# A state-space and attention trunk on one core: the normalization of P from ScalarE to GpSimd

## The chip, the cores and the metric

The kernel runs on one core of a Trainium2 chip. The metric is the device time of one execution in microseconds (us); the median of several runs is compared. The core has five engines with their own instruction streams: TensorE (PE; its weight loads are the rows PEld), VectorE (DVE), ScalarE (ACT), GpSimd (POOL) and SyncE (SP, which only issues transfers here). They run ahead of one another freely and meet through semaphores. An engine works off its stream in order: an instruction that waits holds up all behind it on that engine.

## The reference

512 tokens of 1024 features go through two layers, in float32. Layer 0 is an S5 state-space mixer with a gated projection, then an MLP with squared ReLU (1024 to 4096 to 1024). Layer 1 is sliding-window attention with 16 query heads of 64 over 4 shared key/value heads, then such an MLP, then a final RMSNorm. What the change touches is this part:

```
for each block of 128 queries (4 blocks), against its own and the previous block of keys:
    s = q @ k.T / 8                 # masked to a causal window of 128
    m = maximum(max(s), sink)
    p = exp(s - m)
    denom = sum(p) + exp(sink - m)
    o = (p / denom) @ v
out = o @ w_o + b_o
```

The division p / denom is the normalization that is moved.

## The kernel before, in words

Every large product is made in units. A unit is one panel of 1024 x 128 weights against all 512 tokens. Its 24 matmuls of 128x512 (lines 1110 to 1112, or 1074 to 1076) take each of 8 tiles three times: the weights are split into a high part `w_hi` and a low part `w_lo`, the activations likewise. There are 164 units in a fixed order; PE counts each finished one in `unit_done`. SP brings the panels into two buffers `raw`. POOL makes the two parts, in `split(u, s)`: a tiny `gate()` (line 341), a copy with rounding into `w_hi` (line 414), and after that has landed `w_lo = raw - w_hi` (line 417). There are four slots for the parts, so split u waits until unit u - 4 is done (`unit_done >= u - 3`). Before the change the splits 4 to 163 are one loop on POOL, and POOL does nothing else from unit 4 on.

Attention stands between the units of keys and values (80 to 83), the query units (84 to 91, names `U_Q` and on) and the output units (92 to 99, `U_O` and on). It is cut into 16 steps that the code calls Q, from 0 to 15: Q // 4 says which 4 heads, n = Q % 4 which block of queries. For n = 0 there is no previous block, so a head has 128 keys there and 256 in all other steps. `q = Q % 2` is the buffer. A step has these parts:

- PE `scores(Q)` (line 1205): 8 small matmuls into PSUM. They wait until DVE has read the scores of step Q - 1 (`s_masked`).
- DVE `maxima(Q)`: writes the sink logit into a column of `s_sb` (line 921), adds the mask (line 923), takes the row maximum (929) and negates it (931).
- ACT `exps(Q)` (line 572): one exponential for each of 4 heads, with its row sum.
- DVE `denominators(Q)` (line 936): the reciprocal `rden` of the 4 sums; it counts `rden_done`.
- ACT `norm_p(Q)` (line 579): for each of 4 heads a copy of `s_sb` in place with the per-row scale `rden`; it counts `p_norm`.
- PE `turn_p(Q)` (line 1217): transposes P once `p_norm` has all four counts of the step.
- ACT and DVE `turned(Q)` (lines 585 and 941): each moves half of the transposed P from PSUM to SBUF.
- PE `mix(Q)` (line 1231): P times V. Then ACT `o_hi` (line 591) and DVE `o_low` (line 947) split the result.

The function `skewed` writes the parts out, each engine with its own lags. In pass Q, PE does scores(Q), then dense work that stands beside it, then mix(Q - 2), then turn_p(Q - 1). ACT does turned(Q - 2), o_hi(Q - 3), norm_p(Q - 1), exps(Q). DVE does turned(Q - 2), denominators(Q - 1), maxima(Q), o_low(Q - 3), and in even passes up to 10 the next queries (lines 908 and 910). The dense work is half a query unit (12 matmuls) in each of the passes 0 to 10, half an output unit in passes 11 and 12, none in 13 to 15, and three quarters of a unit each in 16 and 17. Query unit 2 + Q/2 is finished in even pass Q; that is what releases split 90 + Q/2.

Of the kernel before, what the change touches and what calls it, by code (L numbers as in the profile page):

```python
# [11 lines left out]
ACT = mybir.ActivationFunctionType  # L12
# [5 lines left out]
KT = D // P  # L18
# [18 lines left out]
NBLK = L // BLK  # L37
QUADS = 4
# [6 lines left out]
U_Q = U_KV + 4  # L45
U_O = U_Q + KT
NU = U_MLP[1] + 2 * NB_FF * KT
# [50 lines left out]
def build(nc, panels, xu_d, x_d, lam_d, prm_d, dd_d, cst_d, mask_d, col_d, out_d):  # L98
    ctx = ExitStack()
    with ctx:  # L100
        def sb(name, shape, dt=F32, where=ctx):
            return where.enter_context(nc.sbuf_tensor(name, shape, dt))

        def sem(name):
            return ctx.enter_context(nc.semaphore(name))
# [92 lines left out]
        s_sb = sb("s_sb", [P, 2, 4, 2 * BLK + 1], where=over)  # L198
# [4 lines left out]
        rden = sb("rden", [P, 2, 4], where=over)  # L203
# [31 lines left out]
        p_exp, rden_done, p_norm = sem("p_exp"), sem("rden_done"), sem("p_norm")  # L235
# [39 lines left out]
        def window(n):  # L275

            return slice(BLK if n == 0 else 0, 2 * BLK)
# [57 lines left out]
        def _(pool):  # L335
            mul, add, sub = ALU.mult, ALU.add, ALU.subtract
# [73 lines left out]
            def split(u, s):  # L410
                pool.wait_ge(raw_in[s % 2], 16 * (u // 2 + 1) if isinstance(u, int) else 8 * (u - s) + 16 * (s // 2 + 1))
                wait(pool, unit_done, u - 3)
                gate()
                nc.gpsimd.tensor_scalar(w_hi[:, s, :], raw[:, s % 2, :], 1.0, 0.0, ALU.mult, ALU.add  # L414
                                        ).then_inc(w_hi_done, 1)
                pool.wait_ge(w_hi_done, u + 1)
                nc.gpsimd.tensor_tensor(w_lo[:, s, :], raw[:, s % 2, :], w_hi[:, s, :].bitcast(F32),  # L417
                                        ALU.subtract).then_inc(w_split, 1)
# [4 lines left out]
            wait(pool, st_done, 2 * NO)  # L423
            split(2, 2)
            split(3, 3)
            with pool.Fori(1, NU // 4) as i:
                for s in range(4):
                    split(4 * i + s, s)

# [2 lines left out]
        def _(a):  # L432
            act_fn = nc.scalar.activation
# [138 lines left out]
                    act_fn(s_sb[:, q, j, at], s_sb[:, q, j, at], ACT.Exp, bias=negm[:, q, j:j + 1],  # L572
                           accum_out=den[:, q, j:j + 1]).then_inc(p_exp, 1)

            def norm_p(Q):
                u, n, q = Q // NBLK, Q % NBLK, Q % 2
                a.wait_ge(rden_done, Q + 1)
                for j in range(4):
                    act_fn(s_sb[:, q, j, window(n)], s_sb[:, q, j, window(n)], ACT.Copy,
                           scale=rden[:, q, j:j + 1]).then_inc(p_norm, 1)  # L580

            def turned(Q):
                u, n, q = Q // NBLK, Q % NBLK, Q % 2
                a.wait_ge(pt_mm, Q + 1)
                act_fn(pT[:, q, 0:2].rearrange("p t b n -> p t (b n)")[:, :, window(n)],
                       ps[:, 4, :].rearrange("p (t m) -> p t m", t=2)[:, :, window(n)], ACT.Copy).then_inc(pt_a, 1)

            def o_hi(Q):
# [3 lines left out]
                       ps[:, 6 + q, 0:256].rearrange("p (t n) -> p t n", t=2),  # L592
                       ACT.Copy).then_inc(ot_hi, 1)

            skewed([(turned, 2), (o_hi, 3), (norm_p, 1), (exps, 0)])

            with a.Fori(0, KT) as m:
                norm_hi(H_O + 1 + m, m, [("g_mlp1", act)])
# [666 lines left out]
def skewed(stages):  # L1265

    last = QUADS * NBLK
    longest = max(lag for _, lag in stages if lag is not None)  # L1270
    for Q in range(last + longest):
        for stage, lag in stages:
            if lag is None:
                stage(Q)
            elif 0 <= Q - lag < last:
                stage(Q - lag)
# [110 lines left out]
```

## Time and profile before

| what | value |
|---|---|
| median of 3 runs | 1096.73 us (1095.37 to 1097.85) |
| the profiled execution | 1094.58 us, its span 1092.8 us |
| PE busy | 1036.5 us, 95% of the span |
| POOL busy | 721.2 us, 66% |
| DVE busy | 627.4 us, 57% |
| ACT busy | 208.9 us, 19% |

The span is the part of the execution that the profile covers. The attention steps run from 585 us (first scores) to 686 us (last mix); the rest of the span is the state-space part, the gated projection and the two MLPs. A row of a group of instructions tells how many there are and how long one takes; a row of the timeline is one instruction, or several alike in a row; what stands in brackets is how long the engine sat idle before it and which instruction ended that. An idle time with "issue" has no releaser in the profile.

### The profile page before, as it was taken

What the parts mean: (1) busy time and instruction counts of PE and PEld (TensorE: products, weight loads), DVE (VectorE), ACT (ScalarE), POOL (GpSimd) and SP (SyncE); (2) the same over time, 40 slices, a digit from 0 to 9 for tenths busy, and PEclk for the clock granted to TensorE, in tenths of its full rate; (3) what the DMA queues carried; (4) which work ended last, traced back from release to release, by engine and by line L of the source; (5) the groups of instructions that cost most, each with busy time, mean ns of one, the idle gap of its engine ahead of it and who ended that gap; (6) DMA issues with size and microseconds to landing.
All of it is one profiled execution on the core that took longest, in us unless ns stands there. A gap on an engine that the chain in (4) does not pass through costs nothing.

```text
span 1092.8 us, 15893 instructions
## 1 busy us (share of the span) xinstructions
PE 1036.5 (95%) x5640; PEld 845.7 (77%) x5640; DVE 627.4 (57%) x715; ACT 208.9 (19%) x455; POOL 721.2 (66%) x563
## 2 busy tenths in 40 slices
PE   4889999999999999999989998969999999999995
PEld 1778888888888888888877776858888888888884
DVE  7997575687316415615945885767771372273164
ACT  4763121111001000001202776111110010010000
POOL 6997787597667667767845320767776676676650
PEclk9799999999999999999999998989999999999998
DMA  6113332232222222222212110122322222222211
GB/s 239 33 30 98 104 113 96 77 116 96 97 96 97 96 96 97 97 96 97 96 62 93 43 55 1 59 96 78 115 96 97 97 96 97 96 96 97 96 58 77
DMA packets 34863, 97.50 MB, mean 89 GB/s; under 512 B 11136, under 2 KB 11648, under 8 KB 34560
## 3 DMA queue, kind: packets, MB, share of 16 engines
q1 hardware_dynamic: 34816, 96.85, 26.1%
q8 instruction: 33, 0.54, 0.2%
q14 instruction: 14, 0.11, 0.0%
HBM read 92.37 MB, written 2.10 MB: 86 GB/s over the span
## 4 chain that ended last, share of the span: by engine, by line
PE 84%; DVE 9%; issue 3%; ACT 1%; POOL 1%; DMA 1%; DVEq 1%; SPq 0%
PE ps L1110 24%; PE ps L1111 24%; PE ps L1112 24%; PE ps L1074 2%; PE ps L1075 2%; PE ps L1076 2%; PE ps L1217 1%; PE ps L1231 1%; PE ps L1205 1%; DVE t L803 1%; DVE act L809 1%; ACT s_sb L572 1%; DMA prm<-prm_in 1%; DVE h L963 1%; DVE h L980 0%
## 5 line engine op out<-in xcount | busy, mean ns | idle before, releaser
L417 POOL TENSOR_TENSOR w_lo<-raw,w_hi 128x1024 fp32r<-128x1024 f32 x164 | 421.3, 2569 | 13.7
L1110 PE MATMUL ps<-hid,w_hi 128*128 128x512 f32 x736 | 289.2, 393 | 1.9 <-issue 1.9
L1112 PE MATMUL ps<-hid,w_lo 128*128 128x512 f32 x736 | 287.1, 390 | 0.0
L1111 PE MATMUL ps<-hid,w_hi 128*128 128x512 f32 x736 | 287.0, 390 | 0.0
L341 POOL TENSOR_TENSOR gate_sb<-gate_sb 128x1 f32<-128x1 f32 x164 | 42.8, 261 | 316.6 <-PE ps L1112 270.8
L1110 PE MATMUL ps<-act,w_hi 128*128 128x512 f32 x464 | 180.7, 389 | 2.3 <-DVE act L809 2.3
L414 POOL TENSOR_SCALAR w_hi<-raw 128x1024 fp32r<-128x1024 f32 x164 | 182.8, 1114 | 0.0
L1112 PE MATMUL ps<-act,w_lo 128*128 128x512 f32 x464 | 180.5, 389 | 0.0
L1111 PE MATMUL ps<-act,w_hi 128*128 128x512 f32 x464 | 180.5, 389 | 0.0
L868 DVE TENSOR_TENSOR h<-ps,h 128x512 f32 x64 | 44.1, 690 | 227.5 <-PE ps L1112 227.5
L1110 PEld LDWEIGHTS ps<-hid,w_hi 128*128 128x128 f32 x736 | 138.5, 188 | 34.7 <-issue 5.2
L1112 PEld LDWEIGHTS ps<-hid,w_lo 128*128 128x128 f32 x736 | 138.5, 188 | 29.1
L1111 PEld LDWEIGHTS ps<-hid,w_hi 128*128 128x128 f32 x736 | 138.6, 188 | 28.2
L857 DVE TENSOR_TENSOR hid<-t,hid 128x512 fp32r<-128x512 f32 x64 | 129.2, 2019 | 44.7 <-ACT hid L552 44.7
L552 ACT ACTIVATE hid<-t 128x512 fp32r<-128x512 f32 x64 | 40.5, 633 | 455.6 <-DVE t L855 455.6
L1110 PEld LDWEIGHTS ps<-act,w_hi 128*128 128x128 f32 x464 | 87.1, 188 | 20.9 <-DVE act L809 2.7
L1112 PEld LDWEIGHTS ps<-act,w_lo 128*128 128x128 f32 x464 | 87.1, 188 | 18.0
L1111 PEld LDWEIGHTS ps<-act,w_hi 128*128 128x128 f32 x464 | 87.1, 188 | 18.0
L853 DVE SCALAR_TENSOR_TENSOR t<-ps,rstd 128x512 f32<-128x512 f32 x64 | 44.1, 689 | 55.2 <-PE ps L1112 54.7
L855 DVE TENSOR_TENSOR t<-t 128x512 f32<-128x512 f32 x64 | 67.1, 1048 | 2.2
L806 DVE TENSOR_TENSOR acc<-acc,t 128x512 f32<-128x512 f32 x32 | 62.9, 1967 | 3.2
L526 ACT ACTIVATE act<-h,col x24 | 17.4, 724 | 143.3 <-DVEq L870 78.7
(200 smaller groups left out, 1011.9 us busy)
## 6 DMA issues: line engine op xcount, KB each, us to landing
raw<-panels_in SPq DMA_DIRECT2D x164, 512.0 KB, 3.2
xy<-xu_in SPq DMA_DIRECT2D x4, 512.0 KB, 7.9
out<-h SPq DMA_DIRECT2D x8, 256.0 KB, 2.0
prm<-prm_in SPq DMA_DIRECT2D x1, 1280.0 KB, 5.8
h<-x_rows_in SPq DMA_DIRECT2D x1, 1280.0 KB, 13.1
h<-x_rows_in SPq DMA_DIRECT2D x1, 768.0 KB, 7.3
dd<-dd_in SPq DMA_DIRECT2D x1, 256.0 KB, 6.2
toep<-k_even SPq DMA_DIRECT2D x4, 64.0 KB, 2.3
```

Source lines behind the costliest of these rows:

```text
L341: nc.gpsimd.tensor_tensor(gate_sb[:, 0:1], gate_sb[:, 1:2], gate_sb[:, 1:2], ALU.mult)
L414: nc.gpsimd.tensor_scalar(w_hi[:, s, :], raw[:, s % 2, :], 1.0, 0.0, ALU.mult, ALU.add).then_inc(w_hi_done, 1)
L417: nc.gpsimd.tensor_tensor(w_lo[:, s, :], raw[:, s % 2, :], w_hi[:, s, :].bitcast(F32), ALU.subtract).then_inc(w_split, 1)
L552: act_fn(hid[:, par, 0, m, :], t2[:, m % 2, :], ACT.Copy).then_inc(hid_hi, 1)
L806: tt(acc[:], acc[:], t1[:], ALU.add).then_inc(sq_acc, 1)
L853: stt(t1[:], ps[:, m % 4, :], 0.0, rstd[:], ALU.max, ALU.mult).then_inc(bank_free, 1)
L855: tt(t2[:, m % 2, :], t1[:], t1[:], ALU.mult).then_inc(hid_sq, 1)
L857: tt(hid[:, par, 1, m, :], t2[:, m % 2, :], hid[:, par, 0, m, :].bitcast(F32), ALU.subtract).then_inc(hid_lo, 1)
L868: tt(tile(h, m), ps[:, s, :], tile(h, m), ALU.add).then_inc(bank_free, 1)
L1110: mm(ps[:, bank, :], w_hi[:, s, w], x[:, 0, k, :], start=(k == 0), stop=False)
L1111: mm(ps[:, bank, :], w_hi[:, s, w], x[:, 1, k, :], start=False, stop=False)
L1112: last = mm(ps[:, bank, :], w_lo[:, s, w], x[:, 0, k, :], start=False, stop=(k == KT - 1))
```

## The change

The four copies with a scale of `norm_p` leave ACT and become four `tensor_scalar` multiplications on POOL, with the same `rden` as a per-row scalar. For this, POOL's loop over splits is cut at attention: the splits 4 to 83 stay a loop, 84 to 89 are written out, then come 16 passes, each with norm_p(Q) and, in the even passes 0 to 10, split 90 + Q/2 in front of it; the splits 96 to 163 are a loop again. ACT's order in a pass becomes turned(Q - 2), o_hi(Q - 3), exps(Q). PE and DVE keep their streams; turn_p(Q) waits for the same count, which POOL now gives.

```diff
-            with pool.Fori(1, NU // 4) as i:
+            with pool.Fori(1, U_Q // 4) as i:
+                for s in range(4):
+                    split(4 * i + s, s)
+
+            def norm_p(Q):
+                n, q = Q % NBLK, Q % 2
+                pool.wait_ge(rden_done, Q + 1)
+                for j in range(4):
+                    nc.gpsimd.tensor_scalar(s_sb[:, q, j, window(n)], s_sb[:, q, j, window(n)], rden[:, q, j:j + 1], None,
+                                            mul).then_inc(p_norm, 1)
+
+
+            for u in range(U_Q, U_Q + 6):
+                split(u, u % 4)
+            for Q in range(QUADS * NBLK):
+                if Q % 2 == 0 and Q // 2 < KT - 2:
+                    u = U_Q + 6 + Q // 2
+                    split(u, u % 4)
+                norm_p(Q)
+            with pool.Fori((U_O + 4) // 4, NU // 4) as i:
                 for s in range(4):
                     split(4 * i + s, s)
...
-            def norm_p(Q):
-                u, n, q = Q // NBLK, Q % NBLK, Q % 2
-                a.wait_ge(rden_done, Q + 1)
-                for j in range(4):
-                    act_fn(s_sb[:, q, j, window(n)], s_sb[:, q, j, window(n)], ACT.Copy,
-                           scale=rden[:, q, j:j + 1]).then_inc(p_norm, 1)
-
...
-            skewed([(turned, 2), (o_hi, 3), (norm_p, 1), (exps, 0)])
+            skewed([(turned, 2), (o_hi, 3), (exps, 0)])
```

## Rows read from the trace of the kernel before

**Rows 1.** The page's chain that ended last, shares of the span by engine.

```profile
PE 84%; DVE 9%; issue 3%; ACT 1%; POOL 1%; DMA 1%; DVEq 1%; SPq 0%
```

**Rows 2.** Waits of PE in 584 to 690 us: total us, times, longest.

```profile
PE ps L1217 <- ACT s_sb L579: 2.8, 3, 1.2
PE ps L1231 <- ACT pT L585: 2.3, 1, 2.3
```

**Rows 3.** Windows: length; PE, PEld, DVE, ACT, POOL busy (count); PEclk; DMA share; GB/s.

```profile
607.00:659.00 52.00, 52.00 (x378) 39.24 (x376) 40.62 (x73) 39.51 (x134) 14.54 (x12) 1.00 0.12 41
...
667.00:674.00 7.00, 6.52 (x39) 5.12 (x40) 4.81 (x8) 4.85 (x16) 0.00 (x0) 0.57 0.00 0
```

**Rows 4.** Groups of POOL by shape: count, busy us, mean ns, idle before.

```profile
L341 POOL TENSOR_TENSOR gate_sb<-gate_sb 128x1 f32<-128x1 f32 x164 | 42.8, 261 | 316.6 <-PE ps L1112 270.8 <-PE ps L1076 30.3 <-DMA raw<-panels_in 8.2
L382 POOL TENSOR_TENSOR dd<-dd 128x256 f32<-128x256 f32 x1 | 0.7, 732 | 0.0
```

**Rows 5.** Timeline of POOL, splits 90 and 91: start, us, instruction, idle before.

```profile
589.23 0.20 POOL L341 TENSOR_TENSOR gate_sb<-gate_sb 128x1 f32<-128x1 f32 x1 [2.58 <-PE ps L1112]
589.38 1.05 POOL L414 TENSOR_SCALAR w_hi<-raw 128x1024 fp32r<-128x1024 f32 x1
590.51 2.44 POOL L417 TENSOR_TENSOR w_lo<-raw,w_hi 128x1024 fp32r<-128x1024 f32 x1
598.45 0.19 POOL L341 TENSOR_TENSOR gate_sb<-gate_sb 128x1 f32<-128x1 f32 x1 [5.50 <-PE ps L1112]
```

**Rows 6.** Timeline of ACT: norm_p(0), turned(12), norm_p(13), exps(14).

```profile
590.96 1.28 ACT L579 ACTIVATE s_sb<-s_sb,rden 128x128 f32<-128x128 f32 x4 [1.08 <-DVE rden L936]
...
665.20 0.36 ACT L585 ACTIVATE pT<-ps 128x256 f32<-128x256 f32 x1
665.73 1.70 ACT L579 ACTIVATE s_sb<-s_sb,rden 128x256 f32<-128x256 f32 x4
668.18 0.51 ACT L572 ACTIVATE s_sb<-s_sb,negm 128x257 f32<-128x257 f32 x1 [0.76 <-DVE negm L931]
```

**Rows 7.** Timeline of DVE: reciprocals, sink and mask writes, a negation.

```profile
590.84 2.15 DVE L921 TENSOR_SCALAR s_sb<-col 128x4 f32<-128x4 f32 x1
592.90 1.21 DVE L923 TENSOR_TENSOR s_sb<-ps,mask 128x1024 f32<-128x1024 f32 x1
...
597.72 0.18 DVE L936 RECIPROCAL rden<-den 128x4 f32<-128x4 f32 x1 [1.82 <-ACT s_sb L572]
600.37 1.75 DVE L931 TENSOR_SCALAR negm<-mx 128x4 f32<-128x4 f32 x1
...
665.33 0.18 DVE L936 RECIPROCAL rden<-den 128x4 f32<-128x4 f32 x1 [1.49 <-ACT s_sb L572]
```

**Rows 8.** Timeline of PE: turn_p(0), scores(2), turn_p(1), turn_p(2), turn_p(13).

```profile
593.00 0.60 PE L1217 MATMUL ps<-cst,s_sb 128*128 128x128 f32 x4
594.21 1.13 PE L1205 MATMUL ps<-kT,qT 64*128 64x256 f32 x8 [0.62 <-issue]
599.69 1.09 PE L1217 MATMUL ps<-cst,s_sb 128*128 128x128 f32 x8 [0.80 <-ACT s_sb L579]
606.63 1.09 PE L1217 MATMUL ps<-cst,s_sb 128*128 128x128 f32 x8 [0.77 <-ACT s_sb L579]
667.48 1.97 PE L1217 MATMUL ps<-cst,s_sb 128*128 128x128 f32 x8 [1.21 <-ACT s_sb L579]
```

**Rows 9.** Timeline of passes 10 to 12: split 95, sink write, transposes of step 10.

```profile
647.46 2.43 POOL L417 TENSOR_TENSOR w_lo<-raw,w_hi 128x1024 fp32r<-128x1024 f32 x1
648.43 1.49 DVE L921 TENSOR_SCALAR s_sb<-col 128x4 f32<-128x4 f32 x1
652.63 1.09 PE L1217 MATMUL ps<-cst,s_sb 128*128 128x128 f32 x8
```

**Rows 10.** Timeline of the output units: POOL and DVE at one hand-over.

```profile
694.02 0.64 POOL L341 TENSOR_TENSOR gate_sb<-gate_sb 128x1 f32<-128x1 f32 x1
...
691.94 2.68 DVE L806 TENSOR_TENSOR acc<-acc,t 128x512 f32<-128x512 f32 x1
```

## The prediction, made before the kernel was run

> **What bounds the kernel now.** I read the page's chain of work that ended last first: 84% of the span is PE's [rows 1]. PE is busy for 95% of the span, so an edit is worth what it takes off PE's waits and no more. POOL at 66% and ACT at 19% have room as whole engines; what decides is the order of single events in the 100 us of attention. For these the windows come next: from 607 to 659 us PE is busy for 52.00 of 52.00 us at the full granted clock [rows 3]. So in that stretch P's normalization is hidden already, whoever does it. Then the waits of PE in attention: the transposes wait for the normalized P three times, 2.8 us in all, and one mix waits 2.3 us for ACT's half of the transposed P [rows 2]. The first three of these, in the timeline of PE, are 0.80 us before turn_p(1), 0.77 before turn_p(2), 1.21 before turn_p(13) [rows 8]. Before scores(2) PE stands 0.62 us, and that is a wait for DVE's mask of step 1, which ends at 592.90 + 1.21 = 594.11 [rows 7, 8]. That is all the change can win directly: 2.8 us, less what POOL itself needs.
>
> **The change part by part.**
>
> *The price of one norm.* ACT takes 1.70 us for four heads of 256 keys and 1.28 for four of 128 [rows 6]. No row shows POOL's multiplication by a per-row scalar. Nearest is its copy with two constants, 1.05 us for 1024 elements [rows 5], with 0.20 for a single element (the gate in the same rows): slope (1.05 - 0.20) / 1023 = 0.83 ns an element, so 0.20 + 0.21 = 0.41 us for 256 and 0.31 for 128. Four make 1.6 us (n > 0) and 1.2 us (n = 0). I take this value, since shape and kind (one tensor input) are nearest. From below: consecutive starts on POOL lie closer than durations (589.23 to 589.38 is 0.15 for a gate of 0.20 [rows 5]), so 0.36 each, 1.4 us. From above: POOL's only 256-wide instruction has two tensor inputs and takes 732 ns [rows 4]; four are 2.9 us, and for 128 keys (732 + 200) / 2 = 0.47, four 1.9 us. That bound is kept for the range and for a rival.
>
> The Trainium skill bears on this (GPSIMD Engine Reference, "Elementwise — side-by-side cycle accounting"): one-input bodies run at about 1.03 cycles an element, two-input ones at about 2.6. By the first, an estimate for 256 elements at 1.2 GHz is 0.22 us plus dispatch, by the second 0.55 plus dispatch; the page does not say to which kind the per-row scalar belongs.
>
> *What ACT's stream gains.* norm_p went away between o_hi and exps, but exps waits for DVE's negation: before exps(14), ACT stood idle 0.76 us after norm_p(13) and began only when negm came [rows 6]. So the 16 norms, 12 x 1.70 + 4 x 1.28 = 25.5 us of ACT's busy time, were hidden in such waits and leave a hole that nothing fills. Worth 0. The wait of mix(12), 2.3 us [rows 2], is for turned(12), which stands behind exps(13) in ACT's order at 665.20 [rows 6]; exps(13) waits for the negation, so this wait stays.
>
> *Head of the line on POOL.* In even passes up to 10 a split stands before the norm, and it waits for a query unit, not for P. At step 0 the split runs from 589.23 to 590.51 + 2.44 = 592.95 [rows 5]. ACT began norm_p(0) at 590.96 and ended 592.24 [rows 6]; POOL begins at 592.95 and ends at 594.2. turn_p(0) goes from 593.00 to 594.2, and takes 0.6, so scores(2) starts at about 594.85 instead of 594.21 [rows 8]: +0.6, since 0.6 of the delay fills the old wait for the mask.
>
> *Step 1.* rden(1) is there at 597.72 + 0.18 = 597.90 [rows 7]; POOL is free, since split 91 now stands behind: 597.95 to 599.55. PE comes to turn_p(1) at 599.69 - 0.80 + 0.6 = 599.5. It starts at about 599.6, not 599.69: the 0.6 of step 0 is absorbed by the old wait of 0.80. Sum so far -0.1.
>
> *Step 2.* Split 91 starts at 599.55, not at 598.45 [rows 5], and its w_hi runs until 600.75. The negation of step 2 wanted to start at 600.37 and took 1.75 us [rows 7], until w_lo ended; now it meets w_hi and gets in at 600.8, so exps(2) starts 1.1 us earlier. But the queries' scaling behind it (line 910) now meets w_lo and stands until 603.2, and DVE's part of turned(1) and the reciprocal stand behind it: rden(2) about 604.6, norm_p(2) until 606.3, PE there with mix(1) done at 606.3: turn_p(2) 606.35 instead of 606.63. Sum: -0.3 us. Split 91 itself is needed only some 40 us later, and the next panel's transfer has the same room.
>
> *Steps 3 to 12.* Even steps with a split are the tight ones. Step 10: w_lo ends at 647.46 + 2.43 = 649.89, POOL's norm ends at 651.5, PE wants it at 652.63 [rows 9]: 1.1 us of slack; step 6 is the same pattern, steps 4 and 8 (n = 0) have more, and odd steps lose only the 0.1 to 0.3 us for which ACT was still at other copies. 0. By the upper bound of 2.9, step 10 ends at 652.8: +0.2, still nearly covered.
>
> *The port between DVE and POOL.* DVE's sink write, 0.14 us alone, took 2.15 and 1.49 us beside a w_lo [rows 7, 9], and so did the negation: short DVE instructions from SBUF to SBUF stand until POOL's instruction ends. Now four more POOL instructions follow w_lo without a wait between them, and one starts with every reciprocal. The sink write is issued 0.1 us behind the reciprocal and is through before POOL is awake, and the negation comes 2.5 us behind the reciprocal (1.21 + 1.22 + the sink), when a norm of 1.6 us is over. In even steps it depends on who gets the port at a hand-over: at 694.02 DVE's two-input sum had waited since 691.94, and it got in ahead of POOL's gate, which took 0.64 instead of 0.20 [rows 10]. So I take it that the waiting DVE instruction goes first, and price this at 0; if it doesn't, the sink write of steps 1, 5, 7, 9, 11 and 3 stands up to 1.6 us more.
>
> The Trainium skill (SBUF — State Buffer, "SBUF: two separate sides") has a rule that speaks against the change: the shared pair is locked for a whole instruction by whichever starts first. The stretched sink write and negation in this trace agree (2.15 and 1.75 us). By the rule alone each norm instruction can hold DVE for 0.4 us; with all four in a row it is the rival below.
>
> *The end.* Passes 13 to 15 have no dense work, and here the chain through DVE and ACT sets PE. rden(13) is ready at 665.33 + 0.18 = 665.51 [rows 7], but ACT was at turned and o_hi until 665.73 and ended at 667.43 [rows 6]. POOL does it from 665.55 to 667.15: turn_p(13) 0.3 us earlier, and scores(15), on which the last mask waits, with it: -0.25. norm_p(12), (14) and (15) gain nothing: reciprocal, or PE's order, is later.
>
> *The loop written out.* POOL executes the same splits; some 150 instructions now lie in a row, in the time in which POOL idles between splits. 0.
>
> **Sum.** -0.3 and -0.25, about -0.5 us. The profiled execution, 1094.58 us (1092.8 of span and 1.8 around it), would become 1094.1; it lies 2.2 us below the median of the runs, so on the median 1096.73 the forecast is 1096.2 us: no change that shows.
>
> **The rivals.**
>
> *A: POOL's multiplication costs like a two-input instruction.* 2.9 us a norm (1.9 for n = 0). For it: the scalar is a second operand that comes from SBUF. Against: it is read once a row. Then turn_p(0) waits until 594.8, scores(2) is 1.2 late; norm_p(1) ends at 597.95 + 2.9 = 600.85, so turn_p(1) is 1.2 late; norm_p(2), behind the later split, ends near 607.9: +1.3 in all. At the end norm_p(13) runs to 668.45, +1.0. Sum +2.3: 1099.0 us, slower. The point from which it decides: above 0.46 us an instruction the norm passes ACT's time of 1.7 us plus its late start; at 0.72 it is 0.2%.
>
> *B: the port goes to POOL in a row of its instructions.* The sink write of step 1 stands until 594.2, mask and scores(2) come 1.2 late, norm_p(1) too, PE's wait for it stays: +1.1 in the first three steps, +0.2 at step 6, -0.25 at the end: about +1.0, 1097.7 us. For it: no wait separates the four. Against: the hand-over of rows 10.
>
> *C: the clock does not fall at the end.* From 667 to 674 us the granted clock was 0.57, in part the lower of its two levels (1.2 of 2.4 GHz), behind PE's waits of 2.3 and 1.2 us, and the eight transposes took 1.97 instead of 1.09 us [rows 2, 3, 8]. It cost about 6.52 x 0.43 = 2.8 us. If the shift by half a microsecond spares it: -0.5 - 2.8, 1093.4 us, faster. Against: the first wait, of 2.3 us, stays whole.
>
> *D: ACT's freed time is of use after all*, because exps starts 1 us earlier in more steps than I see: at most the 2.8 us of waits go [rows 2]: 1093.9 us.
>
> **How the numbers follow.** What a measurement of this kernel tells from no change is about 0.2%, 2.2 us. Chances: forecast 0.50 (within 1 us of 1096.2), A 0.17, B 0.18, C 0.10, D 0.05. Of A some part stays below 2.2 us and of B and the forecast a small part may go beyond by scatter of the runs (2.5 us among three of them). Faster: C, D and 0.01, 0.16. Slower: most of A and a few of B, 0.18. Within: 0.66. The range reaches down into C and D, 1093.9, and up to A's time with the scatter, 1099.3.
>
> **What would show each step.** Right: L579 gone, four POOL TENSOR_SCALAR of about 0.41 us for 256 keys (0.31 for 128) on a line of norm_p; PE's first transposes start near 594.2, the wait before turn_p(1) under 0.1 us; split 91's gate near 599.5; DVE's sink write in step 11 still near 1.5 us and not 3; the wait for ACT's copy before mix(12) still 2.3 us; the wait before turn_p(13) near 0.9. Wrong: an instruction of 0.6 us or more (A), sink writes of 3 us (B), a granted clock near 1.00 from 667 to 674 us (C), or PE waits that appear between 607 and 659 us, where I count none.

## The result: 1% slower, and the profile after

The changed kernel takes 1106.19 us (1104.41 to 1108.94, 4 runs) against 1096.05 us before: ratio 1.0093, 95% interval 1.0067 to 1.0119, or 10.1 us more. The forecast was 1096.2 us with a range to 1099.3. The price of the norm on GpSimd was wrong by about a factor of two (2.3 for 256 keys, 1.9 for 128), and beyond my upper bound.

PE's waits in attention, of the changed kernel, answer to [rows 2]:

```profile
PE ps L1229 <- POOL s_sb L434: 15.7, 10, 3.0
PE ps L1243 <- ACT pT L597: 1.2, 1, 1.2
```

(Lines have moved: the norm is 434, the transposes 1229, mix 1243, the reciprocal 948, the sink write 933.) Ten steps now wait for P, 15.7 us in place of 2.8. The group of the norm shows why, by shape, with count, busy time and mean ns:

```profile
L434 POOL TENSOR_SCALAR s_sb<-s_sb,rden 128x256 f32<-128x256 f32 x48 | 43.5, 925 | 22.6 <-DVE rden L948 22.6
L434 POOL TENSOR_SCALAR s_sb<-s_sb,rden 128x128 f32<-128x128 f32 x16 | 9.4, 604 | 2.1 <-DVE rden L948 2.1
```

One instruction takes 925 ns for 256 elements where 410 were forecast, and 604 for 128 where 310 were. The windows answer to [rows 3]; behind the length stand the busy times of PE, PEld, DVE, ACT and POOL, each with its count:

```profile
607.00:659.00 52.00, 47.12 (x337) 34.88 (x334) 39.33 (x67) 22.40 (x82) 42.13 (x45) 1.00 0.13 42
```

PE stood idle for 4.9 of 52 us in the stretch where it had been busy throughout, and POOL's busy time went from 14.54 to 42.13 us. How POOL came to set the pace is seen in its timeline of steps 4 to 6 of the changed kernel:

```profile
622.38 2.34 POOL L434 TENSOR_SCALAR s_sb<-s_sb,rden 128x128 f32<-128x128 f32 x4
627.43 3.62 POOL L434 TENSOR_SCALAR s_sb<-s_sb,rden 128x256 f32<-128x256 f32 x4 [2.71 <-DVE rden L948]
631.02 0.46 POOL L341 TENSOR_TENSOR gate_sb<-gate_sb 128x1 f32<-128x1 f32 x1
631.45 1.05 POOL L414 TENSOR_SCALAR w_hi<-raw 128x1024 fp32r<-128x1024 f32 x1
632.58 2.39 POOL L417 TENSOR_TENSOR w_lo<-raw,w_hi 128x1024 fp32r<-128x1024 f32 x1
634.95 3.62 POOL L434 TENSOR_SCALAR s_sb<-s_sb,rden 128x256 f32<-128x256 f32 x4
```

The norm of step 5 begins at 627.43 and its reciprocal is only then there. From that moment POOL works without a gap for 11.1 us: norm 3.6, split 3.9, norm 3.6, to 638.57. PE's transposes of these two steps, 5 and 6:

```profile
631.11 1.09 PE L1229 MATMUL ps<-cst,s_sb 128*128 128x128 f32 x8 [1.08 <-POOL s_sb L434]
...
638.62 1.09 PE L1229 MATMUL ps<-cst,s_sb 128*128 128x128 f32 x8 [1.37 <-POOL s_sb L434]
```

The split finished first, though nothing needed it soon, and P stood behind it. The same pair of waits, 1.1 and 1.4 us, comes again at steps 9 and 10.

The first wait of the pair has a second link. The norm of step 3 (614.94 to 618.56) holds back split 92, so its `w_lo` ends later in step 5 than it did before the change, and DVE's sink write, which stands until `w_lo` ends, takes 1.92 us (its row is shown with rival B below). Before the change it took half of that:

```profile
614.17 0.97 DVE L921 TENSOR_SCALAR s_sb<-col 128x4 f32<-128x4 f32 x1
```

The reciprocal of step 5 comes later by the same 0.95 us, counted from the scores of step 5 (6.57 us after them before, 7.52 now). This chain is read from the rows; no run takes it alone.

A part of the distance between the two profiled executions is not the change's. The first scores and the last mix (step 15) of before, and then of after:

```profile
585.48 0.71 PE L1205 MATMUL ps<-kT,qT 64*128 64x128 f32 x8
...
684.55 0.33 PE L1231 MATMUL ps<-pT,v_sb 128*64 128x128 f32 x2
```

```profile
589.27 0.38 PE L1217 MATMUL ps<-kT,qT 64*128 64x128 f32 x2
...
698.85 0.33 PE L1243 MATMUL ps<-pT,v_sb 128*64 128x128 f32 x2
```

From start to start, attention grew from 99.07 to 109.58 us, by 10.5, close to the 10.1 between the medians. The 3.8 us ahead of it I take for scatter: the eight profiled executions of whole kernels other than this one reached their first scores between 585.2 and 588.0 us, and POOL's program ahead of attention is the same in seven of them. But this one lies 1.3 us outside that spread, so that it is scatter is not shown. Below I use the length from first scores to last mix beside the run times; it comes from one execution of each kernel. Within it, up to the scores of step 12 (start 653.66 before, 665.34 after) 7.9 us are lost, and 2.6 in the end part.

### The profile page after: what moved, and what is told of

It is laid out like the page before. It is cut to its first block, busy times and chain, and to the rows that moved or that the text cites. A ratio compares the mean times of both kernels' runs of the same rounds, so it can differ in the third digit from the quotient of the medians.

```text
span 1107.2 us, 15870 instructions
## 1 busy us (share of the span) xinstructions
PE 1039.9 (94%) x5640; PEld 847.6 (77%) x5640; DVE 628.9 (57%) x715; ACT 185.6 (17%) x391; POOL 773.4 (70%) x627
## 4 chain that ended last, share of the span: by engine, by line
PE 83%; DVE 5%; POOL 5%; issue 2%; ACT 2%; DMA 1%; SPq 0%; DVEq 0%; ACTq 0%
PE ps L1122 23%; PE ps L1123 23%; PE ps L1124 23%; POOL s_sb L434 2%; PE ps L1086 2%; PE ps L1087 2%; PE ps L1088 2%; PE ps L1062 1%; PE ps L1229 1%; PE ps L1074 1%; PE ps L1024 1%; DVE t L815 1%; ACT s_sb L591 1%; PE ps L1055 1%; POOL w_lo L417 1%
## 5 line engine op out<-in xcount | busy, mean ns | idle before, releaser
L434 POOL TENSOR_SCALAR s_sb<-s_sb,rden 128x256 f32<-128x256 f32 (+1 forms) x64 | 52.9, 845 | 24.7 <-DVE rden L948 24.7
```

What stands on the lines that cost most here:

```text
L434: nc.gpsimd.tensor_scalar(s_sb[:, q, j, window(n)], s_sb[:, q, j, window(n)], rden[:, q, j:j + 1], None, mul).then_inc(p_norm, 1)
```

## The experiments

All variants, with the time of one norm for n > 0, the length of attention in the profiled execution, and the ratio to the kernel before:

| kernel | norm, us | attention, us | ratio, 95% interval |
|---|---|---|---|
| before | 1.70 (ACT) | 99.07 | 1 |
| changed | 3.62 | 109.58 | 1.0093 [1.0067, 1.0119] |
| constants (e2) | 1.51 | 97.28 | 0.9978 [0.9963, 0.9993] |
| POOL written out, norm on ACT (e3) | 1.70 (ACT) | 99.05 | 1.0014 [0.9996, 1.0031] |
| norm ahead of the split (e5) | 3.62 | 106.77 | 1.0069 [1.0047, 1.0090] |
| one constant (e8) | 3.29 | 105.33 | 1.0068 [1.0047, 1.0089] |
| times rden, plus 0.0 (e6) | 1.84 | 99.31 | 0.9992 [0.9978, 1.0005] |
| one product for four heads (e4) | 1.90 | 99.64 | 1.0011 [0.9993, 1.0028] |
| e6 with the norm ahead of the split (e7) | 1.84 | 96.38 | 0.9978 [0.9965, 0.9991] |

### A price list of POOL's forms (e1)

```diff
+for w in (128, 256, 512, 1024):
+    ts(b[:, 0:w], a[:, 0:w], 1.0, 0.0, mul, add)
+    ts(b[:, 0:w], a[:, 0:w], 1.0, None, mul)
+    ts(b[:, 0:w], a[:, 0:w], sc[:, 0:1], None, mul)
+    ts(b[:, 0:w], a[:, 0:w], sc[:, 0:1], 0.0, mul, add)     # 128 and 256
...
+ts(a[:, 0:256], a[:, 0:256], sc[:, 0:1], None, mul)          # in place
+ts(odd[:, 1, 0:256], odd[:, 1, 0:256], sc[:, 0:1], None, mul) # rows of 257
```

> A kernel that leaves out the whole computation and only runs single POOL instructions, each waited for before the next, with no other engine busy; one row per form and width. In the changed kernel the norm's multiplication took 0.92 us for 256 elements and 0.60 for 128 (slope 2.5 ns an element, 0.28 fixed), where I had forecast 0.41 and 0.31 from the copy with two constants. Theory P (the per-row scalar from SBUF is what costs): forms with constants take about 0.31 / 0.41 / 1.05 us for 128 / 256 / 1024, the per-row scalar form 0.60 / 0.92 / about 2.8, in place or not, odd row start or not. Theory S (the price lies in the small width, the rows of 257 or the writing in place): constants in place on rows of 257 cost 0.9 too, and the per-row scalar on a plain tile 0.4. Theory D (DVE at work beside it slows it): every 256-wide one-input form here takes 0.4. For a product with a broadcast second tensor I expect a slope near 2.3 ns, so about 2.4 us for 4 x 256 in one instruction.

Groups of POOL by shape. Lines 57 and 59 are two constants and one constant; 61 and 63 are per-row scalar alone and per-row scalar with + 0.0; 65 is in place, 66 on rows of 257; 69 multiplies a tensor by itself, 72 multiplies one by a broadcast second tensor:

```profile
L61 POOL TENSOR_SCALAR b<-a,sc 128x1024 f32<-128x1024 f32 x3 | 8.5, 2842 | 0.3
L59 POOL TENSOR_SCALAR b<-a 128x1024 f32<-128x1024 f32 x3 | 8.3, 2769 | 0.2
L72 POOL TENSOR_TENSOR odd<-odd,sc 128x1024 f32<-128x1024 f32 x3 | 5.7, 1892 | 0.2
L57 POOL TENSOR_SCALAR b<-a 128x1024 f32<-128x1024 f32 x3 | 3.1, 1044 | 0.2
L66 POOL TENSOR_SCALAR odd<-odd,sc 128x256 f32<-128x256 f32 x3 | 2.8, 923 | 0.3
L65 POOL TENSOR_SCALAR a<-a,sc 128x256 f32<-128x256 f32 x3 | 2.8, 922 | 0.3
L61 POOL TENSOR_SCALAR b<-a,sc 128x256 f32<-128x256 f32 x3 | 2.8, 922 | 0.3
L59 POOL TENSOR_SCALAR b<-a 128x256 f32<-128x256 f32 x3 | 2.5, 848 | 0.2
L69 POOL TENSOR_TENSOR b<-a 128x256 f32<-128x256 f32 x3 | 1.8, 612 | 0.2
L61 POOL TENSOR_SCALAR b<-a,sc 128x128 f32<-128x128 f32 x3 | 1.8, 602 | 0.3
L63 POOL TENSOR_SCALAR b<-a,sc 128x256 f32<-128x256 f32 x3 | 1.4, 479 | 0.3
L57 POOL TENSOR_SCALAR b<-a 128x256 f32<-128x256 f32 x3 | 1.2, 404 | 0.2
```

The price of the changed kernel is here too (922 and 602 ns), with no DVE at work, in place or not: theories S and D fall. So does mine, theory P: the per-row scalar adds 922 - 848 = 74 ns to a form with one operation and 479 - 404 = 75 ns to one with two. What costs is that the second operation is absent (the later expectations call this theory F). `times 1.0` alone takes 848 ns for 256 elements, `times 1.0, plus 0.0` 404; from 256 to 1024 elements the slopes are (2769 - 848) / 768 = 2.50 ns and (1044 - 404) / 768 = 0.83 ns an element. The form without is even dearer than a tensor times itself (612) or the two-input instruction of [rows 4] (732). The broadcast product took 1.89 us where I had expected about 2.4.

### Constants in place of rden (e2)

```diff
-tensor_scalar(s_sb[...], s_sb[...], rden[:, q, j:j + 1], None, mul)
+tensor_scalar(s_sb[...], s_sb[...], 1.0, 0.0, mul, add)
```

> The changed kernel with constants (times 1.0, plus 0.0) in place of rden in the norm's four instructions: it leaves the normalization out, all waits and orders stay. Theory P (price of the per-row scalar alone): a norm takes 1.6 us as forecast, and the time returns to what the prediction had, within 1.5 us of the kernel before (1095 to 1097). Theory H (the norm queued behind splits on POOL is what costs, at any price): the time stays 5 us or more above before. Theory B (the port row of four instructions): sink writes of 3 us behind splits and +1 us.

Its norm by shape, and PE's waits in attention:

```profile
L434 POOL TENSOR_SCALAR s_sb<-s_sb 128x256 f32<-128x256 f32 x48 | 18.2, 406 | 35.3 <-DVE rden L948 35.3
PE ps L1243 <- ACT pT L597: 2.5, 1, 2.5
PE ps L1229 <- POOL s_sb L434: 2.4, 5, 1.0
```

With all waits and orders of the change but 406 ns an instruction, the time is 1094.04 us, ratio 0.9978. The price is the cause. At nearly the forecast price the forecast of the steps holds in the main: counted from the first scores, turn_p(0) starts 1.1 us later than before the change, turn_p(1) 0.1 earlier and turn_p(2) 0.7 earlier, where I had 1.2 later, 0.1 and 0.3 earlier; the wait before turn_p(13) is 0.88, where I had 0.9. The total does not quite: the interval runs from -4.1 to -0.8 us, and I had -0.5. Attention came out 1.8 us shorter; a norm took 1.51 us and not 1.6, and at the end the clock rose sooner (below), but no run separates the two. Theory H, order at any price, falls, and so does theory B: no sink write took more than 2.23 us. This run changes two things at once, the scalar and the second operation; e8 and e6 take them apart.

### The program written out, the norm on ACT (e3)

```diff
-with pool.Fori(1, NU // 4) as i: ...
+with pool.Fori(1, U_Q // 4) as i:
...
+for u in range(U_Q, U_Q + 6):
+    split(u, u % 4)
+for Q in range(QUADS * NBLK):
+    if Q % 2 == 0 and Q // 2 < KT - 2:
+        u = U_Q + 6 + Q // 2
+        split(u, u % 4)
+with pool.Fori((U_O + 4) // 4, NU // 4) as i:
...
```

> POOL's splits written out as in the changed kernel, but the norm stays on ACT: the form of the program alone. Theory P and H both expect the time of before, within 1 us. If writing out the program costs (code loading in a critical place), it is above before by more than 2 us, and the 3.8 us by which the changed kernel's profiled execution reached the first scores late would appear here in every execution.

Ratio 1.0014 with one in its interval; attention 99.05 us, first scores at 585.2. Its waits are those of before almost to the digit (2.8, 2.3, 0.7 us). Writing out the splits costs nothing that this can measure.

### The norm ahead of the split (e5)

```diff
-if Q % 2 == 0 and Q // 2 < KT - 2: split(...)
-norm_p(Q)
+norm_p(Q)
+if Q % 2 == 0 and Q // 2 < KT - 2: split(...)
```

> The changed kernel with norm_p(Q) ahead of the split in even passes. The price of 3.6 us a norm stays, the place behind the split goes. If price alone counts, the time stays at the changed kernel's (about +10 over before). If the place behind the split is part of it, the waits of PE before the transposes of steps 0, 2, 6 and 10 (2.3, 1.3, 1.4, 1.4 us) go, and some of those of steps 1, 5, 9 (1.0 to 1.1 each), so 5 to 8 us come back and +3 to +5 stay, nearly all of them from the passes 13 to 15 without dense work, where a norm of 3.6 us is in the chain.

106.77 us of attention, 2.8 less than the changed kernel, and ratio 1.0069. I had expected 5 to 8 us back and 3 to 5 left; 2.7 came back between the medians, 7.6 stay, and the intervals of the two kernels overlap. So the place behind the split is part of the loss, by the trace, and the smaller part. The waits of the even steps 0, 2, 6 and 10 (6.3 us in all) are gone. Of the odd steps, 5 and 9 wait 0.4 us in place of 1.1, but step 1 waits 2.0 in place of 1.0, and 7 and 11 wait 1.4 and 1.2 where they did not wait. POOL's timeline of e5, steps 4 and 5:

```profile
618.25 2.35 POOL L434 TENSOR_SCALAR s_sb<-s_sb,rden 128x128 f32<-128x128 f32 x4 [2.12 <-DVE rden L948]
620.56 0.20 POOL L341 TENSOR_TENSOR gate_sb<-gate_sb 128x1 f32<-128x1 f32 x1
620.72 1.05 POOL L414 TENSOR_SCALAR w_hi<-raw 128x1024 fp32r<-128x1024 f32 x1
621.86 2.37 POOL L417 TENSOR_TENSOR w_lo<-raw,w_hi 128x1024 fp32r<-128x1024 f32 x1
624.22 3.63 POOL L434 TENSOR_SCALAR s_sb<-s_sb,rden 128x256 f32<-128x256 f32 x4
```

The norm of step 5 follows w_lo with no idle time. With 256 keys in both steps, two norms and a split are 11.1 us of POOL, and two passes of PE 11.3 (before, scores(4) starts at 607.66 and scores(6) at 618.93). That leaves 0.2 us, so I don't expect another order to hide it; none was run.

### One constant, no second operation (e8)

```diff
-tensor_scalar(s_sb[...], s_sb[...], rden[:, q, j:j + 1], None, mul)
+tensor_scalar(s_sb[...], s_sb[...], 1.0, None, mul)
```

> The changed kernel with the constant 1.0 alone in the norm's instruction, no second operation: it leaves the normalization out. The price list has 0.85 us for 256 and 0.53 for 128, so 3.4 us a norm without any per-row scalar. Theory F: +8 to +9 over before, next to the changed kernel's +10. Rival P (scalar): as with two constants, 0 to -2.

The group by shape:

```profile
L434 POOL TENSOR_SCALAR s_sb<-s_sb 128x256 f32<-128x256 f32 x48 | 39.5, 849 | 24.1 <-DVE rden L948 24.1
```

No scalar comes from SBUF, and the time is 1.0068 of before, 7.5 us more. Against e2 only the second operation is missing, and that alone is 1.0068 against 0.9978. The 7.5 us are a little under the 8 to 9 that I had put.

### The same values with a second operation (e6)

```diff
-tensor_scalar(s_sb[...], s_sb[...], rden[:, q, j:j + 1], None, mul)
+tensor_scalar(s_sb[...], s_sb[...], rden[:, q, j:j + 1], 0.0, mul, add)
```

> The changed kernel, with the norm's instruction as times rden, plus 0.0, in place of times rden alone: the same values from a form that the price list showed at 0.48 us for 256 and 0.37 for 128, against 0.92 and 0.60. Nothing else differs from the changed kernel. Theory F (the form without a second operation is what costs): four take 1.8 to 1.9 us (1.4 for n = 0), 0.3 more than with constants, and the time comes back to within 1.5 us of before, near 1095 to 1096. Rival P (the per-row scalar costs): the time stays near +10. The wait before turn_p(0) should be about 1.3 us, 0.3 longer than with constants.

```profile
L434 POOL TENSOR_SCALAR s_sb<-s_sb,rden 128x256 f32<-128x256 f32 x48 | 22.1, 481 | 32.9 <-DVE rden L948 32.9
PE ps L1229 <- POOL s_sb L434: 3.6, 5, 1.3
PE ps L1243 <- ACT pT L597: 2.1, 1, 2.1
```

The added second operation takes all of the 10 us back: 1095.35 us, ratio 0.9992 [0.9978, 1.0005]. Against the changed kernel nothing else differs, so theory F is shown. The wait before the first transposes is 1.33 us, as expected. What is left is what the change is worth as it was meant: nothing that this measures. PE's waits agree, 3.6 us for P and 2.1 for the transposed P, 5.7 in all; before it was 2.8, 2.3 and the 0.6 before scores(2), also 5.7.

### One product over four heads (e4)

```diff
-for j in range(4):
-    tensor_scalar(s_sb[:, q, j, window(n)], ..., rden[:, q, j:j + 1], None, mul).then_inc(p_norm, 1)
+tensor_tensor(s_sb[:, q, :, window(n)], s_sb[:, q, :, window(n)],
+              rden[:, q].unsqueeze(2).to_broadcast([P, 4, ...]), mul).then_inc(p_norm, 4)
```

> The changed kernel with one POOL product over the four heads of a step, with rden broadcast over the keys, in place of the four per-row multiplications: 1.89 us for 4 x 256 and 1.04 for 4 x 128 by the price list. Theory F: near the two-operation form, 1095 to 1096. If an instruction of 1.9 us with two tensor inputs holds the port against DVE, the negation and the queries' scaling that meet it stand longer than behind four short ones, and it comes out up to 1 us slower than those.

One instruction of 1.90 us, as the list had it. Ratio 1.0011 [0.9993, 1.0028], attention 99.64 us, against 0.9992 and 99.31 for e6. Whether it is slower than four short ones stays open: the intervals overlap.

### Two operations, and the norm first (e7)

```diff
+norm_p(Q)                      # tensor_scalar(..., rden[...], 0.0, mul, add)
 if Q % 2 == 0 and Q // 2 < KT - 2: split(...)
-norm_p(Q)
```

> The two-operation form with norm_p(Q) ahead of the split in even passes. At the price of 3.6 us this order took about 3 us off. At 1.8 us there is slack behind the splits of steps 4 to 10, so only the wait before turn_p(0) (1.3 us) should go: 0 to 1.3 us faster than the two-operation form in the changed kernel's order. Against it: the splits start later and their w_lo then meets DVE's negation in full, as in the kernel before.

1094.01 us, ratio 0.9978 [0.9965, 0.9991]: this beats both kernels, by about 2.4 us against before. Against e6, which has the other order, the medians lie 1.3 us apart and the intervals overlap; the length of attention differs by 2.9. Waits of PE, and the start of attention in the timeline, both of e7:

```profile
PE ps L1243 <- ACT pT L597: 2.1, 1, 2.1
PE ps L1229 <- POOL s_sb L434: 1.1, 2, 0.8
```

```profile
590.55 0.14 DVE L933 TENSOR_SCALAR s_sb<-col 128x4 f32<-128x4 f32 x1
...
590.74 1.42 POOL L434 TENSOR_SCALAR s_sb<-s_sb,rden 128x128 f32<-128x128 f32 x4 [4.01 <-DVE rden L948]
...
592.12 0.19 POOL L341 TENSOR_TENSOR gate_sb<-gate_sb 128x1 f32<-128x1 f32 x1
...
593.02 0.60 PE L1229 MATMUL ps<-cst,s_sb 128*128 128x128 f32 x4
593.55 1.13 PE L1217 MATMUL ps<-kT,qT 64*128 64x256 f32 x8
...
598.16 1.09 PE L1229 MATMUL ps<-cst,s_sb 128*128 128x128 f32 x8
...
604.26 1.09 PE L1229 MATMUL ps<-cst,s_sb 128*128 128x128 f32 x8
```

All three waits at the start (0.62, 0.80, 0.77 us [rows 8]) are gone, and the steps to the scores of 12 take 65.8 us in place of 68.2. The norm ahead of the split does two things. P is ready when PE comes; and the sink write of step 1 takes 0.14 us and not 2.15 [rows 7]. `w_lo` is not running yet, so the mask and everything behind it come earlier. The same holds in later steps: from step 1 on, no sink write of e7 takes more than 0.22 us, and five in e6 take 1.0 to 2.2. I had expected only the first effect. That the sink write has its share is read from these rows; no run took it alone.

## Why the prediction was wrong, point by point

- *The price of one norm: this is the step that failed.* I took 0.41 us from the copy with two constants, "nearest in shape and kind", and bounded it above by the two-tensor instruction, 0.73. Measured: 0.92. The row I took differed in the one thing that mattered, the second operation, which looked like nothing because it adds 0.0. The upper bound was no bound: it rested on the thought that more operands cost more. The Trainium skill (GPSIMD Engine Reference, "Elementwise — side-by-side cycle accounting") puts a body with k ≤ 2, which I read as up to two operations an element, at 1.03 cycles an element; at the page's 1.2 GHz that is an estimate of 0.86 ns. The two-operation form agrees with 0.83 ns. The one-operation form, with 2.50, is three times as slow and does not, and the measurement decides.
- *Steps 0 to 2*, -0.3: near the price I took, e2 has -0.7 and e6, at 0.48 us an instruction, 0.0.
- *Steps 3 to 12, priced at 0.* Right at the price I took: no transposes of steps 3 to 11 wait in e2 or e6, and e6 needs 68.18 us from the first scores to those of step 12, before 68.18. At 3.62 they cost 5.4 of the 7.9 us (from the scores of step 4 to those of 12). I tested each norm alone against its slack (1.1 us at step 10). In a row, the rows of before show what the dear price does: rden(5) is there at 620.05, and 3.62 + 3.72 + 3.62 us of norm, split and norm end at 631.01, where PE came to turn_p(6) at 629.63. That is 1.38 us late, and 1.37 was measured. At my upper bound, 2.9, the same rows give 629.71, 0.1 late. So the missing sum would not have moved the range; the price would.
- *The port between DVE and POOL, priced at 0.* Right at the price I took: the sink writes of steps 5, 7, 9 and 11 take 1.08, 1.50, 1.03 and 1.49 us in e6, before 0.97, 1.41, 0.97 and 1.49. In the changed kernel they take 1.92 to 2.00, because the norm holds back the split.
- *Rival A* (a dear instruction) was right in its kind, wrong in cause and size: the scalar operand is 75 ns, a norm took 3.6 us and not 2.9, and +10.1 us came of it and not +2.3. It had 0.17.
- *Rival B* (the port goes to POOL's row) is wrong: behind w_lo of split 92 (begun at 620.01, 2.38 us long), DVE's sink write ended at 622.43, while the norm ran from 622.38 to 624.72. The timeline of DVE in the changed kernel, step 5's sink write and mask, shows that DVE's waiting instruction is not held by the norm's row; at steps 1, 3, 7, 9 and 11 too it ends within 0.1 us of the end of `w_lo`:

```profile
620.51 1.92 DVE L933 TENSOR_SCALAR s_sb<-col 128x4 f32<-128x4 f32 x1
622.34 1.21 DVE L935 TENSOR_TENSOR s_sb<-ps,mask 128x1024 f32<-128x1024 f32 x1
```

- *Rival C*: the clock still fell at the end, in e6 and e7 as before (granted 0.50 from 668 to 672 us in e6, behind 4 us in which PE was busy for 0.76; from 664 to 668 in e7). Nothing here spared it; in e2 it rose sooner, and mix(13) took 1.10 us where it had taken 1.89 before.
- *ACT's gain of 0* and *the loop written out, 0*: right. ACT's busy time fell from 208.9 to 185.6 us, and e6, which has the changed kernel's ACT stream, is no faster than the kernel before, so rival D did not come true; the wait for ACT's half of the transposed P is 2.1 us there, before 2.3. e3 shows the second.
- *Head of the line at step 0* (+0.6): right in kind. At the intended price turn_p(0) waited 0.98 us in e2, 1.33 in e6; and e7, which takes it away, is the only version with the whole computation that wins.
- *The end*, -0.25: of 7.9 + 2.6 us, 2.6 were lost here, from the scores of step 12 on, where a norm of 3.6 us is in the chain through the last mask; the longest wait is 3.0 us, before turn_p(13), against 1.21 [rows 8].

## What to carry to other kernels

Before work moves to another engine, the price of that exact form of instruction has to come from a row of that form, or be measured by itself: two forms that compute the same differed here by a factor of two. An upper bound from "something harder" is not a bound. And where an in-order engine gets urgent work among work with slack, add up its row between two deadlines, and try the urgent piece first. Here the order alone was worth 2.8 us of attention at the dear price (109.58 to 106.77) and 2.9 at the cheap one (99.31 to 96.38), in one profiled execution each; between the medians of the runs it was 2.7 and 1.3 us, with intervals that overlap.

## What the hardware showed that was not expected

On POOL, `tensor_scalar` in float32 with one operation (times) costs 2.50 ns an element of a row, with two (times, plus) 0.83: 848 and 404 ns for 256, 2769 and 1044 for 1024. A tensor times itself costs (1892 - 612) / 768 = 1.67. A per-row scalar adds 73 to 75 ns, at every width from 128 to 1024. Other operations and types were not run. Why the form without a second operation is slower is not shown by these runs.
